# Taking a product of two tiles on GpSimd, between its gathers, instead of on VectorE

## The chip, the cores and the metric

One core of one Trainium2 chip runs the whole program. The metric is the device time of one execution, in microseconds (us). The engines are TensorE (PE in the profile; PEld is its weight load), VectorE (DVE), ScalarE (ACT), GpSimd (POOL) and SyncE (SP). "ACTq", "SPq" and "POOLq" are transfers that these engines issue to the 16 DMA engines.

## The reference, cut to what matters

The program is one layer of a streaming encoder: two attention-like branches, an output projection, and then a retrieval of experts (PEER). Only the last part is touched. For each token and each of 8 heads, two sets of 128 keys are scored, the best 16 pairs are chosen out of 128 x 128 experts, and each expert is one row of `expert_u` and one of `expert_v`:

```
fv, fi = lax.top_k(cand, P_TOPK)
eidx = jnp.take_along_axis(cidx, fi, axis=-1)
g = jax.nn.softmax(fv, axis=-1)
act = jax.nn.gelu(jnp.einsum('thkd,td->thk', expert_u[eidx], xi), approximate=False)
return jnp.einsum('thk,thkd->td', (g * act), expert_v[eidx])
```

There are 1152 tokens (1024 of the prompt and 8 streams of 16), that is nine tiles of 128 tokens, and rows of 1024 float32.

## The kernel before

The retrieval is computed in two ways at once. Six of the nine tiles are gathered: for each token the chosen rows are fetched from memory. The other three tiles (`DENSE`, 384 tokens) are dense: all 16384 experts are multiplied, as 128 groups of 128, and a matrix of gates that is zero for what was not chosen keeps the right ones.

The gathered part runs in units. A unit `q` is one tile and one head: 16 rows of `expert_u` for each token (`k` from 0 to 15) and then 16 rows of `expert_v`. GpSimd issues one indirect DMA for each of these 32 rows (L2479, 128 x 1024 float32, 512 KB), into a ring of `ROWS` = 12 buffers; the gather of row `r` first waits for `row_used`, that is until VectorE has consumed row `r - 12`. VectorE waits for each row (`row_loaded`), takes its dot product with the token (L2639, in the trace CUSTOM_DVE_ANT_0 and a short read of the accumulator) or adds it, weighted, into one of two sums (L2658 for the first two, L2661). Ahead of a unit's rows VectorE runs `choose(q + 1)`, the two rounds of top 16 and the index arithmetic for the unit that follows (L2549 to L2589). GpSimd adds the two parts of the index itself (L2473). The first three tiles (24 units) run beside the rest of the network; the dense part runs beside the last 24 units.

A dense group `e` takes these steps. ScalarE loads 128 rows each of `expert_u` (`load_u`, 512 KB, four buffers) and `expert_v` (`load_v`, 512 KB, four buffers). TensorE computes `hidden(e)`, 8 products into one PSUM bank (L2260; each appears twice in the trace, 16 records). ScalarE applies gelu to 128 x 384 values into `W[e % 4]` (L2207, `scalar_step`). `vector_step` (L2235) multiplies that tile in place with the gates of the group (`gate`, loaded for four groups at a time, 768 KB, two buffers). TensorE computes `mixed(e)`, 6 products that add up in six banks over all groups (L2269, 12 records). TensorE's own order is hidden(e), then mixed(e - 2), with `LAG` = 2.

What sets the order: each engine runs its own queue in the order of the program, and semaphores tie them. `PER_UNIT` = 5 dense groups belong to one unit, so 120 of the 128 to the 24 units, and 8 are `left` for the end. VectorE takes its five products of a unit after its dot products `k` = 4, 9 and 14 and after its weighted rows 4 and 9. ScalarE takes three of its five gelu steps, then the gelu of the unit's own dot products (L2531, which waits for all 16), then the other two, then the exponentials for the next unit (L2488, which wait for `choose`). In each step ScalarE issues `load_u(e + 4)` and `load_v(e)`, and at every fourth also the gates of the group of four that comes next, once the products of four steps back are done (`w_ready`). After the last unit VectorE takes the products of the 8 groups that are left and then, for the three dense tiles, copies the sums out of PSUM, multiplies and adds (L2690, L2676, L2678), and SyncE stores them.

Of the kernel before, what the change touches and what calls it, by code (L numbers as in the profile page):

```python
# [1819 lines left out]
class Rest:  # L1820
# [46 lines left out]
    UNITS = 2 * (NT - FIRST)  # L1867
# [262 lines left out]
ROWS = 12  # L2130
# [7 lines left out]
class Dense:  # L2138
# [88 lines left out]
            dve.tensor_tensor(self.oneB[:, b % 2], self.dT[:, d, 1, t:t + 4].unsqueeze(2).to_broadcast([P, 4, PK]),  # L2227
                              self.iota[:, 1, :].unsqueeze(1).to_broadcast([P, 4, PK]), ALU.is_equal).then_inc(self.oneB_ready, 1)

    def vector_step(self, dve, e):  # L2230
        g, jj = divmod(e, JG)
        dve.wait_ge(self.act_ready, e + 1)
        dve.wait_ge(self.gate_loaded[g % 2], g // 2 * 16 + 16)
        w = self.W[:, e % 4, :].rearrange("p (u t) -> p u t", u=12)
        dve.tensor_tensor(w, w, self.gate[:, g % 2, :, jj, :], ALU.mult).then_inc(self.w_ready, 1)  # L2235

    def tensor(self, pe):
        ps = self.ps
# [55 lines left out]
def phase_experts(nc, io, keep, later_parts, hT, branchT, modT, A2, ident, ones, score_rows, x1_rows, h2_rows, g2_rows, gate_rows):  # L2294
# [4 lines left out]
    K = TOPK  # L2299
    UNITS = NT * PH  # L2300
    tile_of = lambda q: ORDER[q // PH]
    gathered = [q for q in range(UNITS) if tile_of(q) not in DENSE]
    nth = {q: n for n, q in enumerate(gathered)}
# [3 lines left out]
    with ExitStack() as ctx:  # L2307
# [155 lines left out]

        @block.gpsimd
        def _(pool):
            for q in range(UNITS):
                if q not in nth:
                    continue
                n, j = nth[q], q % 2
                pool.wait_ge(pick_ready, n * 2 + 2)  # L2470
                if n >= 2:
                    pool.wait_ge(row_used, first_row(q) - 2 * K)
                pool.tensor_tensor(eidx[:, j, :], pick_u[:, j, 0, :], pick_u[:, j, 1, :], ALU.add).then_inc(idx_ready, 1)  # L2473
                pool.wait_ge(idx_ready, n + 1)
                for k in range(2 * K):
                    r = first_row(q) + k
                    if r >= ROWS:
                        pool.wait_ge(row_used, r - ROWS + 1)
                    pool.indirect_dma_start(rows[:, r % ROWS, :], None, io["expert_u" if k < K else "expert_v"],  # L2479
                                            bass.IndirectOffsetOnAxis(ap=eidx[:, j, k % K:k % K + 1], axis=0)  # L2480
                                            ).then_inc(row_loaded[r % ROWS], 16)

        @block.scalar
        def _(act):
# [60 lines left out]
        def _(dve):  # L2545
# [83 lines left out]
            def unit(q):  # L2629
                n, j, h = nth[q], q % 2, q % PH  # L2630
                tile = n // PH
                mine = list(steps_in(q))
                first, second = (beats(halves[2 * q + e]) if q < FIRST * PH else iter(()) for e in range(2))
                pace = [side_steps(halves[2 * q + e]) if q < FIRST * PH else 0 for e in range(2)]
                dve.wait_ge(h2_loaded, tile * 16 + 16)
                for k in range(K):
                    r = first_row(q) + k
                    dve.wait_ge(row_loaded[r % ROWS], r // ROWS * 16 + 16)
                    dve.tensor_tensor_reduce(rows[:, r % ROWS, :], rows[:, r % ROWS, :], h2[:, :], 1.0, 0.0, ALU.mult, ALU.add,  # L2639
                                             dot[:, j, k:k + 1]).then_inc(row_used, 1)  # L2640
                    if mine and k in (4, 9, 14):
                        dense.vector_step(dve, mine.pop(0))
                    for _ in range((k + 1) * pace[0] // K - k * pace[0] // K):
                        next(first)
                if q + 1 < UNITS and q != FIRST * PH - 1:
                    normalise(q + 1)
                dve.wait_ge(gelu_ready, n + 1)
                dve.wait_ge(g_ready, q + 1)
                dve.tensor_tensor(wgt[:, j, :], actv[:, j, :], g[:, j, :], ALU.mult).then_inc(wgt_ready, 1)
                dve.wait_ge(wgt_ready, n + 1)  # L2650
                if h == 0 and tile:
                    dve.wait_ge(stored, tile * 16)
                for k in range(K):
                    r = first_row(q) + K + k
                    own = acc[:, k % 2, :]
                    dve.wait_ge(row_loaded[r % ROWS], r // ROWS * 16 + 16)
                    if h == 0 and k < 2:
                        dve.tensor_scalar(own, rows[:, r % ROWS, :], wgt[:, j, k:k + 1], None, ALU.mult).then_inc(row_used, 1)  # L2658
                    else:
                        dve.wait_ge(row_used, r - 1 if k >= 2 else first_row(q))  # L2660
                        dve.scalar_tensor_tensor(own, rows[:, r % ROWS, :], wgt[:, j, k:k + 1], own,  # L2661
                                                 ALU.mult, ALU.add).then_inc(row_used, 1)
                    if mine and k in (4, 9, 14):
                        dense.vector_step(dve, mine.pop(0))
                    for _ in range((k + 1) * pace[1] // K - k * pace[1] // K):
                        next(second)
                while mine:
                    dense.vector_step(dve, mine.pop(0))

            def finish(n, sums):  # L2670
                out = acc[:, 0, :]
# [25 lines left out]
            for q in range(UNITS):  # L2697
# [15 lines left out]
                if q == FIRST * PH - 1:  # L2713
# [1 line left out]
                        pass  # L2715
                    choose(q + 1)
                    normalise(q + 1)
            for e in left:
                dense.vector_step(dve, e)
            for d in range(3):  # L2720
                dense_sums(n, d)
                n += 1
# [169 lines left out]
```

## Time and profile before

| | |
|---|---|
| three runs | 4881.58, 4904.0, 4908.69 us; median 4904.0 us |
| the profiled execution | 4896.8 us, of which 4894.9 us from the first to the last instruction |
| busy over the span | PE 75%, DVE 64%, POOL 39%, ACT 15% |
| granted clock of TensorE, mean | 0.82 |
| read and written | 1186.43 MB by DMA, 242 GB/s over the span |
| gathers | 1536, 805.40 MB, 43.4% of the DMA engines' time |

The shares are means over very different stretches. The dense part stands in the last third of the span (from about 3400 us), and only that third has the instructions that the change moves. There the page's slices show the DMA engines busy in nine tenths or more and PE too, while POOL and DVE stand at six to eight tenths.

### The profile page before, as it was taken

To read this page: it belongs to the slowest core of one execution; us is meant where nothing else is said; L and a number is where in the kernel's file an instruction comes from. 1 tells how busy PE (TensorE), PEld (TensorE's weight loads), DVE (VectorE), ACT (ScalarE), POOL (GpSimd) and SP (SyncE) were. 2 spreads that over 40 slices of the span, in tenths; PEclk is the share of its full clock that TensorE was granted. 3 is DMA by queue.
4 is the path that set the end of the run, shared out by engine and by line. 5 is a ranking of instruction groups with operands and counts; after the bars stand their busy time and mean duration, and the time that the engine had idled before them with its cause. 6 is when DMAs were issued, how large, how long until landed. Compare 5 with 4: busy or idle time off the path is not lost.

```text
span 4894.9 us, 36868 instructions
## 1 busy us (share of the span) xinstructions
PE 3684.4 (75%) x11160; PEld 2076.4 (42%) x11160; DVE 3119.7 (64%) x6614; ACT 728.7 (15%) x1215; POOL 1923.4 (39%) x1615
## 2 busy tenths in 40 slices
PE   7897879958957777437896653046999999989997
PEld 2443555345534444224453332035444444444443
DVE  1132121031128898997788757998988888888872
ACT  1032100011012333121110211034010001000000
POOL 0000000000007676776566550010777676767760
PEclk9995669958975666559998776579999999999998
DMA  6101220022358888987788782046999999999993
GB/s 246 37 29 49 97 75 26 17 78 80 92 177 316 308 329 308 350 321 276 273 315 322 261 291 87 14 140 214 388 405 408 400 409 400 409 403 406 404 408 127
DMA packets 391103, 1186.43 MB, mean 242 GB/s; under 512 B 37516, under 2 KB 124172, under 8 KB 386452
## 3 DMA queue, kind: packets, MB, share of 16 engines
q0 software_dynamic: 221184, 805.40, 43.4%
q10 hardware_dynamic: 107456, 211.61, 11.5%
q1 hardware_dynamic: 62304, 167.59, 9.9%
q8 instruction: 64, 1.05, 0.1%
q14 instruction: 95, 0.78, 0.0%
HBM read 1116.50 MB, written 67.96 MB: 242 GB/s over the span
## 4 chain that ended last, share of the span: by engine, by line
DVE 19%; PE 17%; DMA 12%; issue 11%; POOL 10%; ACT 1%; ACTq 0%; SPq 0%; DVEq 0%
POOL expert_rows L2479 10%; DMA expert_rows<-in_expert_v,expert_index 6%; DVE expert_rows L2639 3%; PE ps_all L1950 3%; DVE acc L2661 3%; PE ps_all L2250 2%; PE ps_all L1967 2%; PE ps_all L2000 2%; DMA side<-in_w_blk 2%; PE ps_all L2269 1%; DMA score_rows<-side 1%; PE ps_all L2260 1%; PE ps_all L1940 1%; DMA side<-in_w_oT 1%; DVE hot L2579 1%
## 5 line engine op out<-in xcount | busy, mean ns | idle before, releaser
L2479 POOL DMA_INDIRECT expert_rows<-in_expert_u,expert_index x768 | 935.5, 1218 | 755.4 <-DVE dots L2639 515.7
L2479 POOL DMA_INDIRECT expert_rows<-in_expert_v,expert_index x768 | 956.1, 1245 | 374.5 <-issue 227.9
L2661 DVE SCALAR_TENSOR_TENSOR acc<-expert_rows,weights,acc 128x1024 f32<-128x1024 f32 x756 | 940.4, 1290 | 144.8 <-DMA expert_rows<-in_expert_v,expert_index 142.4
L2639 DVE CUSTOM_DVE_ANT_0 expert_rows<-expert_rows,h_rows_sb 128x1024 f32<-128x1024 f32 x768 | 897.5, 1222 | 35.5 <-DMA expert_rows<-in_expert_u,expert_index 35.0
L2260 PE MATMUL ps_all<-hT,branchT 128*128 128x384 f32 x2048 | 716.9, 506 | 82.8 <-ACT side L2207 68.8
L2269 PE MATMUL ps_all<-branchT,side 128*128 128x512 f32 x1536 | 684.6, 595 | 20.1 <-DMA branchT<-in_expert_vj 16.9
L2260 PEld LDWEIGHTS ps_all<-hT,branchT 128*128 128x128 f32 x2048 | 403.9, 198 | 404.8 <-issue 180.9
L2269 PEld LDWEIGHTS ps_all<-branchT,side 128*128 128x128 f32 x1536 | 291.4, 191 | 368.8 <-issue 320.8
L1017 POOL COPY sel_head<-keep 4x128 f32 x4 | 1.1, 285 | 538.3 <-POOLq L68 436.0
L1950 PE MATMUL ps_all<-hT,side 128*128 128x384 f32 x512 | 178.1, 508 | 35.9 <-DMA side<-in_w_blk 35.9
L590 POOL COPY sel_pair<-keep 8x256 f32 x4 | 1.6, 397 | 499.6 <-POOLq L68 398.6
L2242 PE MATMUL ps_all<-consts,keep 128*128 128x128 f32 x9 | 2.7, 436 | 237.4 <-DVE keep L2710 237.4
L2488 ACT ACTIVATE gates<-best,neg_best 128x16 f32<-128x16 f32 x72 | 22.3, 310 | 1063.8 <-DVE neg_best L2570 1050.0
L2000 PE MATMUL ps_all<-hT,side 128*128 128x384 f32 x256 | 103.8, 573 | 66.8 <-DMA side<-in_w_pqT 62.1
L1950 PEld LDWEIGHTS ps_all<-hT,side 128*128 128x128 f32 x512 | 100.7, 199 | 112.5 <-issue 36.7
L2250 PE MATMUL ps_all<-keep 128*128 128x128 f32 x768 | 110.2, 287 | 48.0 <-issue 44.9
L374 PE MATMUL ps_blkA<-hT,w_ringA 128*128 128x384 f32 x384 | 126.9, 494 | 20.0 <-DMA w_ringA<-in_w_blk 20.0
L1599 PE MATMUL ps_all<-consts,side 128*128 128x128 f32 x240 | 59.5, 420 | 107.9 <-ACT side L1699 107.9
L2473 POOL TENSOR_TENSOR expert_index<-picked 128x16 uint32<-128x16 uint32 x48 | 21.4, 446 | 291.2 <-DVE picked L2585 290.4
L383 PE MATMUL ps_rowB<-w_rowsB,hT 128*128 128x512 f32 x288 | 126.8, 603 | 8.0 <-DMA w_rowsB<-in_w_row 8.0
L374 PE MATMUL ps_blkB<-hT,w_ringB 128*128 128x384 f32 x384 | 125.7, 491 | 6.3 <-DMA w_ringB<-in_w_blk 6.3
L2207 ACT ACTIVATE side<-ps_all 128x384 f32<-128x384 f32 x128 | 60.1, 488 | 424.0 <-PE ps_all L2260 423.8
(375 smaller groups left out, 5078.7 us busy)
## 6 DMA issues: line engine op xcount, KB each, us to landing
branchT<-in_expert_uT ACTq DMA_DIRECT2D x128, 512.0 KB, 7.2
branchT<-in_expert_vj ACTq DMA_DIRECT2D x128, 512.0 KB, 9.6
w_mod_ring<-in_w_mod SPq DMA_DIRECT2D x12, 2048.0 KB, 10.1
gate_rows<-branchT ACTq DMA_DIRECT2D x12, 2048.0 KB, 8.7
keep<-gate_rows ACTq DMA_DIRECT2D x32, 768.0 KB, 12.6
expert_rows<-in_expert_u,expert_index POOLq DMA_INDIRECT x768, 8.9
expert_rows<-in_expert_v,expert_index POOLq DMA_INDIRECT x768, 8.9
w_gate_ring<-in_w_blk SPq DMA_DIRECT2D x20, 512.0 KB, 3.6
```

The costliest lines, as they stand in the source:

```text
L374: mm = pe.matmul(ps[:, j, c, 0:TC], w[:, j, k, :], hT[:, k, c * TC:(c + 1) * TC], start=(k == 0), stop=(k == KD - 1))
L383: mm = pe.matmul(ps_row[:, (r * NT + t) % 2, :], hT[:, k, t * P:(t + 1) * P], wr[:, k, :], start=(k == 0), stop=(k == KD - 1))
L1950: mm = pe.matmul(ps[:, 2 * j + c, 0:TC], self.w[:, k, :], hT[:, k, (c + 1) * TC:(c + 2) * TC], start=(k == 0), stop=(k == KD - 1))
L1967: mm = pe.matmul(ps[:, 2 * j + c, 0:TC], self.w[:, k, :], mT[:, k, 0:TC], start=(k == 0), stop=(k == KD - 1))
L2000: mm = pe.matmul(ps[:, c, 0:TC], self.w[:, k, :], hT[:, k, (c + 1) * TC:(c + 2) * TC], start=(k == 0), stop=(k == KD - 1))
L2207: act.activation(self.W[:, e % 4, :], self.ps[:, e % 2, 0:TC], ACT.Gelu).then_inc(self.act_ready, 1)
L2250: mm = pe.matmul(ps[:, b % 4, n * PK:(n + 1) * PK], self.oneA[:, b % 2, n, :], self.oneB[:, b % 2, n, :], start=True, stop=True)
L2260: mm = pe.matmul(ps[:, e % 2, 0:TC], self.uT[:, e % 4, k, :], self.hT[:, k, 2 * TC:T], start=(k == 0), stop=(k == KD - 1))
L2269: mm = pe.matmul(ps[:, 2 + 2 * d + c, :], self.W[:, e % 4, d * P:(d + 1) * P], self.vj[:, e % 4, c * 512:(c + 1) * 512], start=(e == 0), s ...
L2479: pool.indirect_dma_start(rows[:, r % ROWS, :], None, io["expert_u" if k < K else "expert_v"], bass.IndirectOffsetOnAxis(ap=eidx[:, j, k % ...
L2639: dve.tensor_tensor_reduce(rows[:, r % ROWS, :], rows[:, r % ROWS, :], h2[:, :], 1.0, 0.0, ALU.mult, ALU.add, dot[:, j, k:k + 1]).then_inc ...
L2661: dve.scalar_tensor_tensor(own, rows[:, r % ROWS, :], wgt[:, j, k:k + 1], own, ALU.mult, ALU.add).then_inc(row_used, 1)
```

## The change

The product of a dense group (L2235) is issued by GpSimd and not by VectorE: `vector_step` becomes `pool_step`, with the same two waits (gelu done, gates loaded), the same operands and the same signal. In GpSimd's queue it stands right behind the gather of the row that is 12 rows after the one behind which VectorE took it: behind the gathers of weighted rows 0, 5 and 10 of the unit, and of dot rows 0 and 5 of the next one. What falls behind the last gather, and the 8 groups that are left, come at the end of the queue. VectorE's queue keeps nothing in their place.

```diff
-    def vector_step(self, dve, e):
+    def pool_step(self, pool, e):
         g, jj = divmod(e, JG)
-        dve.wait_ge(self.act_ready, e + 1)
-        dve.wait_ge(self.gate_loaded[g % 2], g // 2 * 16 + 16)
+        pool.wait_ge(self.act_ready, e + 1)
+        pool.wait_ge(self.gate_loaded[g % 2], g // 2 * 16 + 16)
         w = self.W[:, e % 4, :].rearrange("p (u t) -> p u t", u=12)
-        dve.tensor_tensor(w, w, self.gate[:, g % 2, :, jj, :], ALU.mult).then_inc(self.w_ready, 1)
+        pool.tensor_tensor(w, w, self.gate[:, g % 2, :, jj, :], ALU.mult).then_inc(self.w_ready, 1)
...
         @block.gpsimd
         def _(pool):
-            for q in range(UNITS):
-                if q not in nth:
-                    continue
+            due = {}
+            for q in gathered:
+                mine = list(steps_in(q))
+                for n, e in enumerate(mine):
+                    at = (4, 9, 14, K + 4, K + 9)[n]
+                    due.setdefault(first_row(q) + at + ROWS, []).append(e)
+            for q in gathered:
                 n, j = nth[q], q % 2
...
                     pool.indirect_dma_start(rows[:, r % ROWS, :], None, io["expert_u" if k < K else "expert_v"],
                                             bass.IndirectOffsetOnAxis(ap=eidx[:, j, k % K:k % K + 1], axis=0)
                                             ).then_inc(row_loaded[r % ROWS], 16)
+                    for e in due.pop(r, ()):
+                        dense.pool_step(pool, e)
+            for r in sorted(due):
+                for e in due[r]:
+                    dense.pool_step(pool, e)
+            for e in left:
+                dense.pool_step(pool, e)
...
-                    if mine and k in (4, 9, 14):
-                        dense.vector_step(dve, mine.pop(0))
...
-                    if mine and k in (4, 9, 14):
-                        dense.vector_step(dve, mine.pop(0))
...
-                while mine:
-                    dense.vector_step(dve, mine.pop(0))
...
-            for e in left:
-                dense.vector_step(dve, e)
```

## Rows read from the trace of the kernel before

**Rows 1.** Stage by stage: PE, PEld, DVE, ACT, POOL busy, clock, DMA share, GB/s.
```profile
3440.00:4780.00 1340.00, 1252.06 (x3282) 636.62 (x3282) 1155.23 (x2117) 122.84 (x228) 942.54 (x766) 0.97 1.02 405
```

**Rows 2.** The same columns in windows of 4 us; three units, at the weighted rows.
```profile
3658.00:3662.00 4.00, 4.00 (x10) 1.72 (x10) 3.84 (x9) 0.59 (x2) 3.13 (x3) 1.00 0.95 349
...
4007.00:4011.00 4.00, 4.00 (x11) 1.85 (x10) 3.08 (x9) 0.60 (x2) 3.08 (x4) 1.00 1.02 405
...
4121.60:4125.60 4.00, 4.00 (x11) 1.74 (x10) 3.93 (x10) 0.59 (x2) 3.09 (x4) 1.00 0.88 257
...
4702.00:4706.00 4.00, 4.00 (x13) 2.12 (x12) 4.00 (x4) 0.00 (x0) 3.09 (x3) 1.00 0.97 363
```

**Rows 3.** Waits from 3440 to 4780 us: us in total, times, longest.
```profile
POOL expert_rows L2479 <- DVE dots L2639: 158.3, 28, 12.3
...
PE ps_all L2260 <- ACT side L2207: 68.8, 20, 9.2
...
DVE acc L2661 <- DMA expert_rows<-in_expert_v,expert_index: 136.4, 135, 2.8
```

**Rows 4.** POOL in order of time: start, us; in brackets the idle time before.
```profile
3470.79 1.68 POOL L2479 DMA_INDIRECT expert_rows<-in_expert_u,expert_index  x1 [5.85 <-DVE dots L2639]
...
3980.56 0.94 POOL L2479 DMA_INDIRECT expert_rows<-in_expert_u,expert_index  x1 [0.30 <-issue]
...
3991.87 1.99 POOL L2479 DMA_INDIRECT expert_rows<-in_expert_u,expert_index  x1 [0.30 <-issue]
3994.16 1.32 POOL L2479 DMA_INDIRECT expert_rows<-in_expert_u,expert_index  x1 [0.30 <-issue]
3995.79 1.98 POOL L2479 DMA_INDIRECT expert_rows<-in_expert_u,expert_index  x1 [0.30 <-issue]
3998.07 1.98 POOL L2479 DMA_INDIRECT expert_rows<-in_expert_v,expert_index  x1 [0.30 <-issue]
```

**Rows 5.** DVE in order of time, the same unit, around one product.
```profile
3994.11 0.56 DVE L2235 TENSOR_TENSOR side<-side,keep 128x384 f32<-128x384 f32 x1
3994.58 1.22 DVE L2639 CUSTOM_DVE_ANT_0 expert_rows<-expert_rows,h_rows_sb 128x1024 f32<-128x1024 f32 x1
...
3995.73 1.22 DVE L2639 CUSTOM_DVE_ANT_0 expert_rows<-expert_rows,h_rows_sb 128x1024 f32<-128x1024 f32 x1
```

**Rows 6.** POOL's other instructions, from their lines: shortest/median/longest ns.
```profile
L1415 POOL COPY head_keys<-sub_keys x8: 295/296/297, 1391.1 to 1431.1; 128x128 f32 x8
...
L1336 POOL COPY gate_tiles<-modT x1: 1037/1037/1037, 1362.2 to 1362.2; 128x1024 f32<-128x1024 f32 x1
...
L2473 POOL TENSOR_TENSOR expert_index<-picked x48: 217/379/1842, 1464.9 to 4714.8; 128x16 uint32<-128x16 uint32 x48
```

**Rows 7.** PE and ACT in order of time, the same unit.
```profile
3988.03 7.09 PE L2260 MATMUL ps_all<-hT,branchT 128*128 128x384 f32 x16 [3.08 <-ACT side L2207]
3995.28 5.39 PE L2269 MATMUL ps_all<-branchT,side 128*128 128x512 f32 x12 [0.16 <-DMA branchT<-in_expert_vj]
4000.51 5.32 PE L2260 MATMUL ps_all<-hT,branchT 128*128 128x384 f32 x16
4005.67 5.31 PE L2269 MATMUL ps_all<-branchT,side 128*128 128x512 f32 x12
...
4009.76 0.47 ACT L2207 ACTIVATE side<-ps_all 128x384 f32<-128x384 f32 x1
```

**Rows 8.** The start of the dense part: DVE and POOL in order, one window.
```profile
3423.00 0.56 DVE L2235 TENSOR_TENSOR side<-side,keep 128x384 f32<-128x384 f32 x1 [18.53 <-DMA keep<-gate_rows]
...
3424.97 1.68 POOL L2479 DMA_INDIRECT expert_rows<-in_expert_v,expert_index  x1 [17.10 <-DVE dots L2639]
...
3430.00:3435.00 5.00, 5.00 (x16) 2.80 (x16) 5.00 (x9) 0.00 (x0) 4.39 (x3) 1.00 0.76 230
```

**Rows 9.** The end: POOL and PE in order of time.
```profile
4742.14 1.31 POOL L2479 DMA_INDIRECT expert_rows<-in_expert_v,expert_index  x1 [0.31 <-issue]
...
4741.56 5.42 PE L2269 MATMUL ps_all<-branchT,side 128*128 128x512 f32 x12 [1.91 <-DVE side L2235]
```

More of the change, by code:

```diff
@@ L2631, in unit @@
                 tile = n // PH
-                mine = list(steps_in(q))
                 first, second = (beats(halves[2 * q + e]) if q < FIRST * PH else iter(()) for e in range(2))
```

## The prediction

> **What bounds the kernel now.** I read the slices of the page first: only the last third holds the instructions that move. Then the busy time of that stage, from 3440 to 4780 us [rows 1]: the DMA engines are busy for a share of 1.02 and move 405 GB/s, while POOL is busy 943 and DVE 1155 of 1340 us. So the first suspect is DMA bandwidth, and an engine that is relieved gains nothing by itself. TensorE is busy for 1252 us, but its five groups of a unit need only ten steps of 5.16 us from start to start [rows 7], 51.6 us, and a unit lasts about 57 us (23 of them from the first dot product of the first unit to the last weighted rows; 1340 / 57 = 23.5). The difference is what it waits for ScalarE, 68.8 us in 20 waits [rows 3].
>
> Next the same stage in windows of 4 us, since a mean of 405 hides dips [rows 2]. They all lie at one place of a unit, 8 to 16 us after the gather of the first weighted row. In 10 of the 23 units the rate there falls below 400 GB/s; the first (349), one of the deepest (257) and the last (363) are shown, beside a unit that keeps 405. There the DMA engines have nothing left to do for a moment: the bound passes to whoever supplies them.
>
> The supplier is POOL. Its list in order of time shows two speeds [rows 4]: a gather takes 0.94 us and 0.30 to the next, 1.24 in all, while VectorE does little; it takes 1.32 to 1.99 us while VectorE runs dot products back to back, so 1.63 to 2.29 from start to start. For 512 KB in 2.29 us that is 229 GB/s, far under 405. The waits show the rest [rows 3]: POOL stands for VectorE 158.3 us in 28 waits, and that is one wait per unit, when its ring of 12 is full and VectorE is in `choose`; the usual one is 5.85 us [rows 4], 5.55 over the gap that is always there. So POOL has about 5.5 us of room in a unit and no more, all of it at the unit's start. VectorE waits for rows 136.4 us [rows 3], 5.9 us in a unit.
>
> **What leaves VectorE.** 128 products. From the start of one to the next instruction it is 0.47 us (3994.11 to 3994.58 [rows 5]), so 2.35 us in a unit of five. VectorE waits 5.9 us per unit for rows as it is, so this is worth nothing on the path: the wait for the rows grows by what is saved.
>
> **What POOL takes on.** No row has a 128x384 product on POOL. From below: its copies of 128 and of 1024 columns take 0.296 and 1.037 us [rows 6], so 0.83 ns for a column and 0.19 us fixed, and 384 columns 0.51 us if a second input were free. From the nearest two-input row, 0.217 us for 16 columns at its shortest [rows 6], less 0.19: 1.7 ns for a column, 0.84 us for 384. To that comes what slows the gathers: next to VectorE's two-input work one of them is held by up to 1.99 - 0.94 = 1.05 us [rows 4]. So between 0.51 and 1.89 us. I take 1.1: 0.84 and a quarter of 1.05, because a gather that has been held ends about 0.25 us ahead of VectorE's next boundary, and the product stands right behind it.
>
> The rows say that VectorE's two-input work holds POOL up; they do not say the reverse, since dot products follow one another every 1.15 us [rows 5] whatever POOL issues. The Trainium skill has a rule on it ("SBUF — State Buffer", section "Who interferes with whom"): a VectorE instruction with two SBUF inputs and a GpSimd instruction that reads SBUF exclude each other, and whichever starts first keeps the shared ports until it ends. The trace agrees for the half it can show (0.94 against 1.99 us); the other half, POOL's product in front of VectorE, would be new here and is the fourth rival below.
>
> **POOL's account.** Five products are 5.5 us. One thing comes on top: a VectorE product shifts the phase between the two engines, and that is where the short slots of 1.63 us come from (3994.16 to 3995.79 [rows 4], with the product at 3994.11 [rows 5]). Without the three products among the dot products three slots become 2.29, 2.0 us more, and VectorE's busy stretch ends 3 x 0.47 = 1.4 us earlier: 0.6 us net. Together 6.1 us against 5.5 us of room. As a sum it nearly fits, and by the sum alone nothing would be lost.
>
> **The place.** The first product of a unit stands behind the gather of weighted row 0, and that is just ahead of the dip. The room lies before that place, at the unit's start, so there the 1.1 us cannot be taken from it. In the 10 units that run dry the delay goes straight to the DMA engines: 1.1 and 0.6 us. A third part comes by way of TensorE. POOL does the product of group 0 of a unit when the gather behind which it stands is out, at 3998.07 + 1.98 + 1.1 = 4001.2 us in the unit shown [rows 4], where `mixed` started at 3995.28 [rows 7]: 5.9 us later. Then hidden of group 3 ends at 4001.2 + 2 x 5.16 = 4011.5, and ScalarE's gelu of that group, with its 1 MB of loads, moves from 4009.76 [rows 7] to about 4011.7. That is 2 us in which the engines run at 257 and not 405 GB/s [rows 2], 0.7 us. So 2.4 us in each of these 10 units. In the 13 others some backlog is left that no row measures: between nothing and all of 2.4 us, and I take half, 1.2. The sum is 10 x 2.4 + 13 x 1.2 = 40 us.
>
> **What costs nothing.** TensorE is later by 5.9 us within a unit, but it only moves its wait: ten steps are 51.6 us of 57, and its wait for ScalarE (3.08 us and a slow step of 7.09 behind it [rows 7]) becomes a wait for the product. If the unit were shorter than 51.6 us this cover would be gone. POOL's wait for gelu: queued behind it are all later gathers, and VectorE waits for those; but the gelu of a unit's first two groups is done before VectorE's own product, and POOL comes 4 to 9 us after that, so it never waits in mid-stage. ScalarE's wait for `w_ready` ahead of a load of gates asks for products four steps back: nothing. Later products move no DMA of POOL's or SyncE's but the gathers behind them, and those have the backlog of the weighted rows, where a gather takes 1.24 us [rows 4].
>
> **Both ends of the stage.** At the start VectorE stands 18.53 us for the first gates [rows 8], and POOL 17.10 us behind it. In the changed kernel VectorE goes on to consume the rows that have landed, and POOL alone waits, so that at 3424 us it finds an empty ring and issues in 1.24 rather than up to 2.29 us. For some 15 us the engines have room (230 GB/s at 3430 [rows 8]); a third of it is 5 us gained. At the end TensorE runs without a pause from `mixed` of the last unit's first group, 4741.56 us [rows 9]. It will start when POOL is done with it: 4742.14 + 1.31 + 1.1 = 4744.6, 3 us lost.
>
> **The sum.** 40 - 5 + 3 = 38 us. On the profiled execution's 4896.8 us that is 4935 us. The median of the runs shown, 4904.0, lies 7 us above that execution, inside their spread of 27 us, and I make no correction for it. A run of this kernel can tell about 0.5% from no change, 25 us.
>
> **The rivals.**
> All of it is hidden: the 13 units have backlog to spare, and what the 10 lose they get back since POOL's room grows as a unit gets longer. Then only the ends count, -5 + 3: 4895 us. For it speaks the flat 405 GB/s of [rows 1]; against it the dips. Chance 0.26.
>
> POOL becomes the bound: each product loses a full turn to VectorE and costs 1.89 us. 5 x 1.89 + 0.6 = 10.05 against 5.55 us of room makes each of 23 units 4.5 us longer, 104 us, which covers the loss at the place: 4896.8 + 104 - 2 = 4999 us. It decides from a price of 1.3 us or so, when five products pass the room and the 1.2 us. For it: gathers at 1.98 us are the rule, not the exception, in the dot products. Chance 0.15.
>
> VectorE is held up: POOL's product keeps it off for its 0.84 us. Net of the 0.47 that leaves, 5 x 0.37 = 1.85 us in a unit, 43 us in 23 if the 5.9 us of waiting hide none of it, on top of the forecast: 4978 us. The sentence on the skill above is the reason to list it. Against it: most of these products fall where VectorE waits for rows. Chance 0.08.
>
> Faster: VectorE sets the pace after all, being busy for 1155 of 1340 us [rows 1], each unit gets shorter by 2.35 us, 23 x 2.35 = 54 us, and with the ends 4841 us. It decides if the rows land as soon as VectorE frees their buffers. Against it stands a DMA share of 1.02: rows can't come sooner. Chance 0.09.
>
> **How the numbers follow.** The forecast, 4935 us, has a chance of 0.42 and its own range of 4910 to 4970, from a quarter to nearly all of the 2.4 us in the 13 units and the price at 0.84 or 1.4. The range over all reaches down to the hidden case and the spread of a run below it, 4880, and up into the POOL-bound case, 5010; outside are the faster case (0.09) and the dearest part of POOL's and VectorE's (0.06). Slower by over 0.5% is above 4921 us on this execution's scale: 0.42 less the 0.05 of it that lies lower, 0.15 and 0.08, makes 0.60. Faster by as much: 0.09. The rest, 0.31, within.
>
> **What would show it.** Right: the products on POOL's list at 0.8 to 1.4 us; the one wait for VectorE per unit shrunk from 5.85 to about nothing; dips at weighted rows 2 to 5 in nearly all units and deeper; `mixed` of a unit's first group waiting for POOL; units of 58 to 59 us. Wrong: units of 57 us with POOL's room still there (hidden), rows of POOL above 1.8 us with no wait for VectorE at all (POOL-bound), VectorE's dot products further apart than 1.15 us beside a product (VectorE held), or units under 56 us (faster). The step that I trust least is the half for the 13 units.

## The result, and the profile after

The changed kernel takes 4927.0 us in the median of 20 runs (4909.07 to 4943.87), the kernel before 4904.11 in 20 (4881.58 to 4918.86). The medians are 23 us apart. The ratio taken over all the runs is 1.0053 (about 26 us), with a 95% interval of 1.0040 to 1.0067. The profiled execution of it took 4937.08 us. Lines have moved by a few: L2483 is the gather, L2649 the dot product, L2669 the weighted row; L2235, the product, is now GpSimd's.

The page of the changed kernel: the span, busy time by engine, and the product's group.

```profile
span 4935.2 us, 36868 instructions
PE 3696.9 (75%) x11160; PEld 2073.3 (42%) x11160; DVE 3145.1 (64%) x6486; ACT 730.0 (15%) x1215; POOL 2073.2 (42%) x1743
...
L2235 POOL TENSOR_TENSOR side<-side,keep 128x384 f32<-128x384 f32 x128 | 143.4, 1121 | 83.7 <-ACT side L2207 74.5
```

The stage from 3440 to 4780 us, columns as in [rows 1]: 395 GB/s where it was 405, POOL busier by 137 us, VectorE by 5 although it does no product any more.

```profile
3440.00:4780.00 1340.00, 1225.06 (x3200) 621.08 (x3199) 1160.03 (x1975) 124.03 (x224) 1079.37 (x868) 0.95 1.01 395
```

Waits of the same stage (us in total, times, longest). Against [rows 3], POOL's standing for VectorE has shrunk from 158.3 to 65.5 us, and TensorE waits for POOL's product instead of for ScalarE.

```profile
DVE acc L2669 <- DMA expert_rows<-in_expert_v,expert_index: 129.3, 125, 3.6
...
PE ps_all L2269 <- POOL side L2235: 104.2, 22, 8.5
...
POOL expert_rows L2483 <- DVE dots L2649: 65.5, 41, 9.9
...
PE ps_all L2260 <- ACT side L2207: 10.7, 5, 5.6
```

How long is a unit? I take it from the first dot product of one unit to that of the next. The two lists of VectorE in order of time show the first dot product of the second unit in the dense part and of the last but one; 21 units lie between. Before:

```profile
3469.29 1.22 DVE L2639 CUSTOM_DVE_ANT_0 expert_rows<-expert_rows,h_rows_sb 128x1024 f32<-128x1024 f32 x1
...
4680.12 1.22 DVE L2639 CUSTOM_DVE_ANT_0 expert_rows<-expert_rows,h_rows_sb 128x1024 f32<-128x1024 f32 x1
```

After:

```profile
3473.37 1.22 DVE L2649 CUSTOM_DVE_ANT_0 expert_rows<-expert_rows,h_rows_sb 128x1024 f32<-128x1024 f32 x1
...
4714.48 1.22 DVE L2649 CUSTOM_DVE_ANT_0 expert_rows<-expert_rows,h_rows_sb 128x1024 f32<-128x1024 f32 x1
```

So 1210.8 / 21 = 57.66 us before and 1241.1 / 21 = 59.10 after. With that the 40.3 us between the two spans (4935.2 - 4894.9) fall into four parts: 8.8 us already stand at the first dot product of the dense part (3407.5 against 3398.7), ahead of everything that the change touches, and in the other profiles below this point lies anywhere from 3385 to 3416 us; the first unit is 65.9 and not 70.6 us, -4.7; the 21 units give +30.3; and from 4680.12 and 4714.48 to the end it is 214.8 and 220.7 us, +5.9. Without the first part the change costs 31.5 us in this one execution, inside the interval of the ratio (19.6 to 32.9 us).

The DMA rate in windows, three dips of the changed kernel (columns as in [rows 1]; the unit's first dot product is at 4125.5 and 4185.8 us): one at the weighted rows, as before, and one in two windows at the end of a unit, where the kernel before has none.

```profile
4149.50:4153.50 4.00, 4.00 (x13) 2.24 (x12) 3.85 (x4) 0.49 (x1) 3.08 (x4) 1.00 0.81 264
4229.80:4233.80 4.00, 4.00 (x12) 1.90 (x12) 3.60 (x11) 0.00 (x0) 3.39 (x3) 1.00 0.91 288
4233.80:4237.80 4.00, 4.00 (x12) 2.04 (x11) 3.79 (x16) 0.00 (x0) 3.33 (x4) 1.00 0.86 278
```

### The profile page after: what moved, and what is told of

It is laid out like the page before. It is cut to its first block, busy times and chain, and to the rows that moved or that the text cites. A ratio compares the mean times of both kernels' runs of the same rounds, so it can differ in the third digit from the quotient of the medians.

```text
span 4935.2 us, 36868 instructions
## 1 busy us (share of the span) xinstructions
PE 3696.9 (75%) x11160; PEld 2073.3 (42%) x11160; DVE 3145.1 (64%) x6486; ACT 730.0 (15%) x1215; POOL 2073.2 (42%) x1743
## 4 chain that ended last, share of the span: by engine, by line
DVE 23%; PE 18%; DMA 11%; issue 9%; POOL 8%; ACT 1%; SPq 0%; DVEq 0%; ACTq 0%; POOLq 0%
DVE expert_rows L2649 8%; POOL expert_rows L2483 7%; DMA expert_rows<-in_expert_v,expert_index 5%; PE ps_all L1950 3%; DVE acc L2669 3%; PE ps_all L2250 2%; PE ps_all L1967 2%; PE ps_all L2000 2%; PE ps_all L2260 1%; DMA side<-in_w_blk 1%; PE ps_all L2269 1%; DMA expert_rows<-in_expert_u,expert_index 1%; DMA score_rows<-side 1%; PE ps_all L1940 1%; DMA side<-in_w_oT 1%
## 5 line engine op out<-in xcount | busy, mean ns | idle before, releaser
L2483 POOL DMA_INDIRECT expert_rows<-in_expert_u,expert_index x768 | 951.1, 1238 | 658.3 <-DVE dots L2649 429.7
L2483 POOL DMA_INDIRECT expert_rows<-in_expert_v,expert_index x768 | 944.4, 1230 | 358.6 <-issue 206.9
L2669 DVE SCALAR_TENSOR_TENSOR acc<-expert_rows,weights,acc 128x1024 f32<-128x1024 f32 x756 | 985.3, 1346 | 141.5 <-DMA expert_rows<-in_expert_v,expert_index 138.5
L2649 DVE CUSTOM_DVE_ANT_0 expert_rows<-expert_rows,h_rows_sb 128x1024 f32<-128x1024 f32 x768 | 920.4, 1253 | 41.5 <-DMA expert_rows<-in_expert_u,expert_index 40.9
L2269 PE MATMUL ps_all<-branchT,side 128*128 128x512 f32 x1536 | 719.1, 620 | 106.1 <-POOL side L2235 106.1
L2260 PE MATMUL ps_all<-hT,branchT 128*128 128x384 f32 x2048 | 687.6, 490 | 24.4 <-DMA branchT<-in_expert_uT 13.6
L2260 PEld LDWEIGHTS ps_all<-hT,branchT 128*128 128x128 f32 x2048 | 391.6, 191 | 327.0 <-issue 91.6
L2269 PEld LDWEIGHTS ps_all<-branchT,side 128*128 128x128 f32 x1536 | 303.7, 199 | 478.0 <-issue 330.2
L2235 POOL TENSOR_TENSOR side<-side,keep 128x384 f32<-128x384 f32 x128 | 143.4, 1121 | 83.7 <-ACT side L2207 74.5
L374 PE MATMUL ps_blkA<-hT,w_ringA 128*128 128x384 f32 x384 | 126.7, 494 | 19.8 <-DMA w_ringA<-in_w_blk 19.8
```

The costliest lines, as they stand in the source:

```text
L374: mm = pe.matmul(ps[:, j, c, 0:TC], w[:, j, k, :], hT[:, k, c * TC:(c + 1) * TC], start=(k == 0), stop=(k == KD - 1))
L2235: pool.tensor_tensor(w, w, self.gate[:, g % 2, :, jj, :], ALU.mult).then_inc(self.w_ready, 1)
L2260: mm = pe.matmul(ps[:, e % 2, 0:TC], self.uT[:, e % 4, k, :], self.hT[:, k, 2 * TC:T], start=(k == 0), stop=(k == KD - 1))
L2269: mm = pe.matmul(ps[:, 2 + 2 * d + c, :], self.W[:, e % 4, d * P:(d + 1) * P], self.vj[:, e % 4, c * 512:(c + 1) * 512], start=(e == 0), s ...
```

## The experiments

Three theories stood against each other. *The place*: what counts is the first product of a unit, since it stands ahead of the dip (the prediction). *The sum*: what counts is all that POOL works in a unit, wherever it stands. *The hold*: a product of POOL that reads keeps VectorE off. The table is what the profiles gave. "Unit" is the mean of the same 21 units. "Works" is that length less the time in which POOL stood longer than the gap of 0.30 us that is always there; "stands" is that time. Both are summed over POOL's list in order of time. "Row" is the mean of a weighted row in these units. The ratios are taken over all runs of a kernel and runs of the kernel before that were taken with them; they are close to the quotients of the medians but not equal to them (e9_fill_mid: 3 us between the medians, 1.0019 or 9 us by the ratio).

| kernel | POOL works | stands | unit | row us | ratio, 95% |
|---|---|---|---|---|---|
| before | 50.6 | 7.0 | 57.66 | 1.285 | 1 |
| changed | 56.6 | 2.5 | 59.10 | 1.401 | 1.0053 (1.0040 to 1.0067) |
| e1_both | 56.3 | 2.8 | 59.09 | 1.383 | 1.0028 (1.0008 to 1.0047) |
| e2_fill | 54.2 | 3.4 | 57.67 | 1.284 | 1.0003 (0.9989 to 1.0017) |
| e3_unrelieved | 57.5 | 1.8 | 59.23 | 1.365 | 1.0049 (1.0031 to 1.0068) |
| e4_left_out | 49.4 | 8.3 | 57.66 | 1.280 | 0.9979 (0.9963 to 0.9995) |
| e5_fill_twice | 58.1 | 1.4 | 59.52 | 1.283 | 1.0094 (1.0067 to 1.0122) |
| e6_copy | 56.8 | 2.5 | 59.29 | 1.398 | 1.0071 (1.0044 to 1.0097) |
| e7_first_only | 51.9 | 6.2 | 58.06 | 1.280 | 1.0003 (0.9983 to 1.0023) |
| e8_four_only | 55.5 | 2.5 | 58.02 | 1.365 | 1.0027 (1.0006 to 1.0047) |
| e9_fill_mid | 55.5 | 2.5 | 58.00 | 1.284 | 1.0019 (1.0002 to 1.0036) |
| e10_one_and_early | 50.7 | 7.2 | 57.81 | 1.283 | 0.9997 (0.9982 to 1.0012) |
| e11_end_on_vector | 57.7 | 1.8 | 59.45 | 1.363 | 1.0062 (1.0042 to 1.0082) |
| e12_in_room | 55.8 | 4.2 | 59.99 | 1.281 | 1.0093 (1.0071 to 1.0114) |

A profile is one execution and lies up to 20 us off the median of its kernel, so a unit's length is trusted to some tenths of a us and no further. Part of that lies ahead of the dense part, but not all: from the first dot product of the dense part to the end, e1_both's profile is 28.0 us longer than that of before and e3_unrelieved's 34.7, while their ratios allow 4 to 23 and 15 to 33 us. The other profiles lie inside their intervals.

### POOL's work, and the relief of VectorE

**e1_both**: VectorE keeps its products, and POOL does a second one on spare tiles at the places of the change. **e2_fill**: the same with a fill of equal length, which reads nothing.

```diff
+    def pool_extra(self, pool, e):
+        g = e // JG
+        pool.wait_ge(self.act_ready, e + 1)
+        pool.wait_ge(self.gate_loaded[g % 2], g // 2 * 16 + 16)
+        o = e % 2 * TC
+        pool.wait_ge(self.extra, max(e - 1, 0))
+        pool.tensor_tensor(self.spare[:, o:o + TC], self.spare_in[:, 0:TC], self.spare_in[:, TC:2 * TC], ALU.mult).then_inc(self.extra, 1)
```

```diff
-        pool.tensor_tensor(self.spare[:, o:o + TC], self.spare_in[:, 0:TC], self.spare_in[:, TC:2 * TC], ALU.mult).then_inc(self.extra, 1)
+        pool.memset((self.spare, self.spare_in)[e % 2], 0.0).then_inc(self.extra, 1)
```

> VectorE keeps the real products, where they were; GpSimd takes a second product of the same shape (128x384, two inputs, on unused tiles, with the same two waits) at each place where the changed kernel has its own. So GpSimd pays, VectorE is relieved of nothing, and TensorE gets its tile as early as before. If the loss is GpSimd's delay of the gathers (the forecast): +15 to +30 us against the kernel before, about the changed kernel's +23, less what TensorE's lateness costs (7 us by the forecast) and plus the 5 us that the changed kernel gains at the start. If what counts is VectorE's time, lengthened by shared ports and no longer relieved: the relief of 71 us is missing, +60 us or more.

> As e1_both, but GpSimd fills 128x1152 numbers of unused tiles (it writes and reads nothing) instead of the second product: about as long, 1.06 us by the line through the two fills of the trace. If the loss is the time that GpSimd spends at these places: as e1_both, within 8 us. If it is the shared read ports, VectorE's row instructions at 1.22 us again and the time within 5 us of the kernel before.

POOL's and VectorE's groups of the fill (busy us, mean ns, idle before), then VectorE's of the changed kernel, all from 3440 to 4780 us:

```profile
L2238 POOL MEMSET keep<- 128x1152 f32 x118 | 127.0, 1076 | 0.1
...
L2682 DVE SCALAR_TENSOR_TENSOR acc<-expert_rows,weights,acc 128x1024 f32<-128x1024 f32 x370 | 465.2, 1290 | 127.0 <-DMA expert_rows<-in_expert_v,expert_index 125.6
L2660 DVE CUSTOM_DVE_ANT_0 expert_rows<-expert_rows,h_rows_sb 128x1024 f32<-128x1024 f32 x373 | 437.2, 1220 | 30.3 <-DMA expert_rows<-in_expert_u,expert_index 29.9
```

```profile
L2669 DVE SCALAR_TENSOR_TENSOR acc<-expert_rows,weights,acc 128x1024 f32<-128x1024 f32 x362 | 499.0, 1406 | 131.6 <-DMA expert_rows<-in_expert_v,expert_index 129.3
L2649 DVE CUSTOM_DVE_ANT_0 expert_rows<-expert_rows,h_rows_sb 128x1024 f32<-128x1024 f32 x361 | 443.0, 1285 | 35.0 <-DMA expert_rows<-in_expert_u,expert_index 34.5
```

In its one profile the second product alone makes the units as long as the change does (59.09 and 59.10 us). Over the runs it costs less: 14 us in the medians, a little under what was expected, where the change costs 23. So POOL's product alone costs something, and whether that is all of the change's loss isn't shown. Five fills of 1.08 us at the same places cost nothing, so a delay of 1.1 us ahead of the dip is not by itself what hurts. Beside the fill VectorE's instructions are as long as before (1290 and 1220 ns); beside the product of the changed kernel they are not (1406 and 1285). In e1_both the weighted rows grow too (1.383 us), the dot products hardly (1.237).

**e3_unrelieved**: the changed kernel, with an extra product of VectorE at its old places. **e4_left_out**: nobody does the product.

```diff
+    def vector_extra(self, dve, e):
+        o = e % 2 * TC
+        dve.wait_ge(self.act_ready, e + 1)
+        dve.wait_ge(self.extra, max(e - 1, 0))
+        dve.tensor_tensor(self.spare[:, o:o + TC], self.spare_in[:, 0:TC], self.spare_in[:, TC:2 * TC], ALU.mult).then_inc(self.extra, 1)
```

```diff
-            act.wait_ge(self.w_ready, e // JG * JG)
+            act.wait_ge(self.gate_loaded[(e // JG + 1) % 2], (e // JG + 1) // 2 * 16)
...
-        dve.tensor_tensor(w, w, self.gate[:, g % 2, :, jj, :], ALU.mult).then_inc(self.w_ready, 1)
...
-            pe.wait_ge(self.w_ready, e + 1)
+            pe.wait_ge(self.act_ready, e + 1)
```

> The changed kernel, and VectorE takes a product of the same shape on unused tiles at each place where it took the real one. If VectorE's relief is worth nothing, as forecast: the changed kernel's time, +20 to +30 us. If the relief hides part of the loss: up to 54 us more, +50 to +75.

> The kernel before without the product at all: TensorE multiplies the ungated values as soon as gelu is done. No engine pays. If VectorE's relief is worth nothing in mid-stage: 0 to -10 us (the wait for the first gates at the start goes, about 5 us). If VectorE sets the pace of a unit: -54 us.

The stage of both, in that order:

```profile
3440.00:4780.00 1340.00, 1234.46 (x3196) 624.65 (x3195) 1208.75 (x2084) 124.03 (x225) 1094.15 (x868) 0.95 1.01 395
```

```profile
3440.00:4780.00 1340.00, 1249.22 (x3306) 635.24 (x3305) 1108.80 (x1997) 122.05 (x228) 903.50 (x751) 0.98 1.02 404
```

VectorE's busy time moves by 100 us between them (1209 and 1109), and it decides little: with the relief taken back the changed kernel has units of 59.23 us, and without any product the unit is that of before, 57.66. e4 gains 14 us in the median; its profile shows 8 of them in the first unit (62.6 us, where no product waits for the first gates) and 2 at the end.

### How much POOL can take, and where

**e5_fill_twice** and **e9_fill_mid** fill 2304 and 1664 columns instead of 1152; **e6_copy** copies 1152.

```diff
+        pool.memset(self.spare2, 0.0).then_inc(self.extra, 1)
...
+        pool.tensor_copy(self.spare, self.spare_in).then_inc(self.extra, 1)
```

> e2_fill with twice the length: 128x2304 numbers, about 2.1 us on GpSimd at each of the places, written and nothing read; VectorE keeps the real products. If GpSimd's work in a unit is what counts (in e2_fill 32 issues of 1.53 us, five fills of 1.1 and 0.8 us make about 55 us of 57.4, and so cost nothing): about 60 us, each of 22 units 2.5 us longer, +50 to +60 us. If only reads beside VectorE's row instructions cost: within 5 us of the kernel before.

> e2_fill with 128x1664 numbers, about 1.50 us by the line through the fills of e2_fill and e5_fill_twice: chosen so that GpSimd's work in a unit, 32 issues, the index and five fills, makes 57.1 us, as in e1_both, without a read. If GpSimd's sum is what counts: as e1_both, +10 to +28 us. If it is that GpSimd's reads hold VectorE's weighted rows (1.38 against 1.28 us in e1_both): 0 to +6 us.

> As e2_fill, but a copy of 128x1152 numbers (one input) instead of the fill, 1.15 us by the line through the two copies of the trace. VectorE keeps the real products. If reads of GpSimd beside VectorE's two-input instructions cost: as e1_both, +10 to +25 us, with VectorE's row instructions longer than 1.22 and 1.28 us. If only GpSimd's time counts: within 5 us of e2_fill, that is of the kernel before.

POOL's groups, the double fill and then the copy:

```profile
L2494 POOL DMA_INDIRECT expert_rows<-in_expert_u,expert_index x368 | 438.8, 1192 | 136.1 <-issue 91.6 <-DVE dots L2661 34.2 <-POOL expert_index L2488 6.2
...
L2239 POOL MEMSET keep<- 128x2304 f32 x113 | 230.2, 2037 | 0.1
```

```profile
L2493 POOL DMA_INDIRECT expert_rows<-in_expert_u,expert_index x368 | 452.9, 1231 | 160.1 <-issue 90.5 <-DVE dots L2660 60.5 <-POOL expert_index L2487 6.2
...
L2238 POOL COPY keep<-keep 128x1152 f32<-128x1152 f32 x113 | 144.5, 1279 | 0.5
```

The fills leave VectorE's rows as long as before and so give a ladder: POOL works 54.2, 55.5 and 58.1 us in a unit, and the unit is 57.67, 58.00 and 59.52 us. So POOL's work makes units longer without holding VectorE's rows, from about 55 us on, with 2.5 us of standing still left. Two things grow together on this ladder, the sum and the length of each of the five stretches in which no gather goes out (1.08, 1.50 and 2.04 us); it doesn't tell them apart, and more but shorter fills were not tried. The fill of 1.50 us lies below what the sum was expected to give: 3 us in the medians, 9 by the ratio (1 to 18), against 10 to 28. The copy reads, is shorter than that fill, and costs more (+31 us in the medians, 1.0071). Part of that is POOL's own: its gathers beside the copy take 1.27 us in the mean and beside the fill 1.19, so it works 56.8 us and not 55.5.

**e7_first_only** leaves to POOL only the first product of each unit, the one at *the place*; **e8_four_only** leaves to it the other four and the 8 at the end.

```diff
+    def on_pool(e):
+        return e < 120 and e % 5 == 0
```

```diff
+    def on_pool(e):
+        return e >= 120 or e % 5 > 0
```

> The changed kernel with only the first product of each unit on GpSimd (behind the gather of weighted row 0), the other four and the 8 left over on VectorE. If the place ahead of the dip is what costs (the forecast): most of the changed kernel's loss, +15 to +25 us. If it is the sum of GpSimd's work: one product fits in its room of 5.5 us, and only the late start of TensorE's last stretch stays, 0 to +7 us.

> The opposite: the first product of each unit on VectorE, the other four and the 8 left over on GpSimd. If the place ahead of the dip is what costs: 0 to +8 us. If it is the sum of GpSimd's work: four fifths of it, by the account 1.1 us per unit less than the changed kernel, so 0 to +8 us as well; if it is every product that meets VectorE's rows: +12 to +18 us. With e7_first_only it tells the place from the sum: place 20 and 5, sum 3 and 5, each product alike 5 and 15.

What TensorE waited for, in e7 and then in e8:

```profile
PE ps_all L2288 <- POOL side L2246: 89.5, 23, 8.4
```

```profile
PE ps_all L2288 <- POOL side L2246: 61.2, 23, 5.6
...
PE ps_all L2279 <- ACT side L2208: 21.5, 8, 6.2
```

How deep the dips are can be added up: in windows of 4 us, the bytes that each falls short of 405 GB/s, as the time that they would take at that rate, in 21 units. At the weighted rows (16 to 32 us after a unit's first dot product) that is 11.7 us before and 24.6 changed; in the last 16 us of a unit, 0.2 and 13.7. So about half of the change's loss stands at a place where the kernel before loses nothing. The first product alone makes the dips at the weighted rows deeper (19.8 us; 0.2 at the end) and the units 0.40 us longer; the median hardly moves (+2 us), so these 0.40 us are not clear of the noise. The other four alone make these dips nearly vanish (2.1 us) and open those at the end (11.0 us): the units are 0.36 us longer, and the median is 18 us up (13 by the ratio). Of the accounts that the two runs were to tell apart, the place (20 us in e7 and 5 in e8) falls, since e7's interval is -8 to 11 us. The sum (3 and 5) and a cost for each product alike (5 and 15) both lie inside the two intervals (e8's is 3 to 23), and these runs don't decide between them. All five give 1.44, nearly twice the sum of the two. Where VectorE keeps the products and POOL does something more at the same places, nearly all of the missing time is at the end: 10.5 and 27.1 us in e1_both, 10.1 and 30.7 in e6_copy, 5.1 and 38.6 in e5_fill_twice.

**e12_in_room** takes e1 and moves all five second products behind the gather of dot row 11, where POOL stands anyway because its ring is full.

```diff
-                for n, e in enumerate(mine):
-                    at = (4, 9, 14, K + 4, K + 9)[n]
-                    due.setdefault(first_row(q) + at + ROWS, []).append(e)
+                for e in mine:
+                    due.setdefault(first_row(q) + 2 * K + ROWS - 1, []).append(e)
```

> VectorE keeps the real products. GpSimd does the same second product of 128x384 as in the run with both, five in a unit, but all five behind the gather of dot row 11 of the next unit, where it stands each time because its ring is full. So GpSimd's work in a unit is the same as there (account about 57 us), only its place in the queue is another. If the sum of GpSimd's work is what costs, wherever it stands: units of 58.4 to 58.8 us and 1.002 to 1.005 of the time of before. If the cost comes from the gathers that stand behind a product and go out late, then five products of 1.12 us fit into the 5.5 us of standing there, no gather goes out more than about 1 us late, and it is nothing: units of 57.3 to 57.7 us, GpSimd's wait behind dot row 11 gone, 0.999 to 1.001. If it is VectorE that is held by a product that reads: the products stand beside the choice of the next unit, whose instructions would be longer, and the dot products and weighted rows would go back to the means of before (1.22 and 1.28 us); units of 57.4 us plus what the choice gets longer by, up to 5 x 0.5 us.

POOL and VectorE in order of time, one unit, and in a fence of its own one instruction of `choose` in all units of the stage (shortest/median/longest ns):

```profile
4124.77 4.81 POOL L2239 TENSOR_TENSOR keep<-keep 128x384 f32<-128x384 f32 x5
4133.70 1.72 POOL L2493 DMA_INDIRECT expert_rows<-in_expert_u,expert_index  x1 [4.12 <-DVE dots L2660]
...
4126.35 3.27 DVE L2593 TENSOR_SCALAR best_pair<-best_at 128x16 uint32<-128x16 uint32 x1
4129.53 0.16 DVE L2594 TENSOR_SCALAR best_pair<-best_at 128x16 uint32<-128x16 uint32 x1
```

```profile
L2593 DVE TENSOR_SCALAR best_pair<-best_at x22: 175/3270/4516, 3464.4 to 4723.3; 128x16 uint32<-128x16 uint32 x22
```

The same instruction in the kernel before:

```profile
L2572 DVE TENSOR_SCALAR best_pair<-best_at x22: 174/175/176, 3466.5 to 4677.4; 128x16 uint32<-128x16 uint32 x22
```

The hold came nearest: its units were 57.4 us plus up to 2.5, it expected the rows at their old length (1.281 us), and the unit is 59.99. What is held it had not named. An instruction of 16 columns, 0.175 us before, stands until POOL's train of five products ends (4124.77 + 4.81 = 4129.58), and its twin behind it takes 0.16 again. `choose`, from the last weighted row to the first dot product, goes from 9.06 to 13.40 us in the median, and POOL waits for it once more. So *the hold* is real, and where it hits `choose` it is on the path: the unit is 59.99 us although POOL works 55.8, 2 us longer than e8 or e9 at nearly the same work. Whether the room could be filled with work that reads nothing was not tried as such. But in e5_fill_twice a fill, which only writes, runs into the same instruction in 4 of the 21 units, and holds it too, for up to 1.71 us:

```profile
3931.03 2.04 POOL L2239 MEMSET keep<- 128x2304 f32 x1
...
3931.39 1.71 DVE L2594 TENSOR_SCALAR best_pair<-best_at 128x16 uint32<-128x16 uint32 x1
```

### Two attempts at a better kernel

**e10_one_and_early**: VectorE does the products but the very first, which POOL takes, and ScalarE takes four gelu steps ahead of the unit's own gelu instead of three.

```diff
+    def on_pool(e):
+        return e == 0
...
-                    for e in mine[:3]:
+                    for e in mine[:4]:
...
-                    for e in mine[3:]:
+                    for e in mine[4:]:
```

> A candidate that should beat the kernel before: only the very first of the 128 products on GpSimd (so that GpSimd and not VectorE waits for the first gates; 4.7 us in the changed kernel's first unit), and ScalarE takes the fourth of a unit's gelu steps, with its 1 MB of loads, ahead of the gelu of the unit's own dot products, so that these loads fall into the dip behind the first weighted rows (12 us of missing transfers in 22 units). Both: -5 to -15 us. If the dips are not on the path: -4 us.

ScalarE's wait for the dot products falls from 328.8 us to 66.0, TensorE's wait for ScalarE stays (70.1 us, 68.8 in [rows 3]). The first unit is 68.0 us and not 70.6; the time is that of before, and the 5 to 15 us were not gained.

**e11_end_on_vector**: the changed kernel with the last unit's products and the 8 at the end on VectorE.

```diff
+    def on_pool(e):
+        return e < 115
```

> The changed kernel, with the last unit's five products and the 8 left over on VectorE. If TensorE's last stretch, which starts late when its first product waits for GpSimd, is part of the loss: 5 to 10 us less than the changed kernel, +13 to +18 us. If the loss is all in the units before: +23 us.

It gains nothing. TensorE's last wait, in the changed kernel and then here, is that for the first product of the last but one unit:

```profile
4728.06 7.11 PE L2269 MATMUL ps_all<-branchT,side 128*128 128x512 f32 x12 [4.25 <-POOL side L2235]
```

```profile
4732.46 6.92 PE L2288 MATMUL ps_all<-branchT,side 128*128 128x512 f32 x12 [4.87 <-POOL side L2246]
```

From there TensorE has no wait above 0.3 us, so what comes later on POOL or VectorE can't help it. That answers to [rows 9], where its last wait came a unit later.

## Why the prediction was right, and where it was not

Forecast: 38 us over the profiled execution of before. Measured: 40.3 us there, 31.5 of them in the part that the change touches, and 23 in the medians. The time was right; two steps of its reasons were not.

**POOL's price and account: right.** The product takes 1.121 us in the mean, taken as 1.1. POOL works 6.0 us more in a unit; the account said 6.1.

**"As a sum it nearly fits, and by the sum alone nothing would be lost": this step failed.** The ladder of fills shows that the cost begins about 2.5 us before the room is used up. POOL's room is a mean of 7.0 us, but units differ (5.85 us in the usual one, 12.3 at most [rows 3, 4]): in the changed kernel 6 of the 21 units have nothing left while the mean still has 2.5. The second place where the rate falls, at a unit's end, is worth 13.7 us of full rate in 21 units and was in no term of the sum.

**The place: a part, not the whole.** The forecast put all of 40 us, 1.7 us per unit, on the first product and nothing on the four others, "those have the backlog". Measured, the first alone gives 0.40 us per unit, the four alone 0.36, all together 1.44. Two of its three parts, the 1.1 and 0.6 us that a late gather was to cost, don't show at this place: with POOL as busy there but TensorE's tile on time (e1, e6) the dips are no deeper than before. The third part does: the gelu of a unit's group 3, with its 1 MB of loads, comes 25.2 us after the unit's first dot product in the mean where it was 21.4, so 3.8 us later and not 2, and 24.9 in e7, whose dips are deeper too (in e3 26.0, with 13.9 us missing); in e1 it is 21.9, in e8 21.3. The half for the 13 units was the step trusted least; the dips did become deeper, but in about as many units as before, not in nearly all. That the size came out is luck: too much at this place and nothing at the other offset each other.

**VectorE's relief worth nothing: right,** by e3 and e4. The list of VectorE shows besides that it isn't even relieved: its rows became longer beside POOL's products. Here a dot product beside the product of POOL, 2.00 us instead of 1.22:

```profile
4137.86 1.18 POOL L2235 TENSOR_TENSOR side<-side,keep 128x384 f32<-128x384 f32 x1
4139.18 1.78 POOL L2483 DMA_INDIRECT expert_rows<-in_expert_v,expert_index  x1
...
4136.96 1.22 DVE L2649 CUSTOM_DVE_ANT_0 expert_rows<-expert_rows,h_rows_sb 128x1024 f32<-128x1024 f32 x1
...
4138.11 2.00 DVE L2649 CUSTOM_DVE_ANT_0 expert_rows<-expert_rows,h_rows_sb 128x1024 f32<-128x1024 f32 x1
```

**The start, -5: right** (-4.7). VectorE no longer stands for the first gates; POOL does (its list), and the rate from 3430 us is 411 GB/s where it was 230 [rows 8] (the window):

```profile
3431.95 0.99 POOL L2235 TENSOR_TENSOR side<-side,keep 128x384 f32<-128x384 f32 x1 [12.11 <-ACT side L2207]
```

```profile
3430.00:3435.00 5.00, 3.41 (x10) 1.57 (x9) 1.70 (x2) 0.60 (x2) 2.60 (x3) 1.00 1.02 411
```

Of the others, the runs in which POOL has the first product (e3, e7, e10, e11) have a first unit of 66.6 to 68.0 us, those in which VectorE has it 69.9 to 72.2, and 74.2 in e12.

**The end, +3: too small** (+5.9). `mixed` of a unit's first group starts 13.6 us after the unit's first dot product where it was 7.8, 5.8 us later; the forecast said 5.9 and costed it at nothing, since TensorE has waits to spare. That holds in mid-stage. After the last but one unit there are none, and the 5.8 us fall due. The wait of 1.91 us that TensorE still had in the kernel before [rows 9] would have taken up a part, but the step behind the late start ran 7.11 us (the line under e11_end_on_vector) and not 5.31.

**The rivals.** *Hidden* and *faster* fall: units are longer. *POOL becomes the bound* was nearer the mechanism but had the wrong price (1.89 us, measured 1.121) and the wrong point from which it decides: not when five products pass the room, at a price of 1.3 us, but from about 55 us of work in the fills, and then gently. *VectorE held*: the hold is there, and so is the sign that the forecast named for it, dot products further apart than 1.15 us beside a product (the lines above), but how much of the 1.44 us it makes stays open. At POOL's work of 56.6 us the ladder of fills, read in a straight line between 55.5 and 58.1, gives a unit of 58.6; the changed kernel has 59.1. The 0.5 us that are left may be the hold, or the product's place and size; and POOL's work contains gathers that VectorE holds in turn.

## What to carry to other kernels

In this kernel the engine that issues the gathers had less room than its waits showed: compare what it works in a unit with the unit's length, and expect a cost when a few us are left, not when none is. Work that was moved to GpSimd cost twice where it read, once on GpSimd and once on the VectorE instructions beside it, so a relief of VectorE is best counted in the lengths that VectorE shows afterwards. A phase shift that waits absorb in every unit can fall due after the last wait.

## What the hardware showed unexpectedly

**The hold goes both ways, and for VectorE's rows only reading counts.** Beside products of POOL dot products rose from 1.224 to 1.285 us and weighted rows from 1.290 to 1.406 in the mean; beside fills of the same length they stayed. An integer instruction of 16 columns (a tensor_scalar) was held by reading and writing alike: 1.71 us instead of 0.175 beside a fill, until the fill ended, and 3.27 us in a train of POOL's products. The Trainium skill ("SBUF — State Buffer", section "Who interferes with whom") says that a VectorE instruction with two SBUF inputs collides with a GpSimd one that reads but not with one that only writes, that a tensor_scalar can collide too, and that whichever starts first blocks the other entirely; these rows agree. The train goes further than that sentence: the integer instruction started at 4126.35, while the second of the five products ran (0.96 us each from 4124.77), and was let in only behind the fifth.

**A pause of TensorE shows in its clock.** After it waited 6.70 us for POOL, a step of `mixed` took 8.41 us (5.39 in [rows 7]), and in the 4 us from 4141.5 the granted clock was 0.54 of full speed, so for nearly all of them the lower of its two levels, 1.2 GHz of 2.4. The list and the window:

```profile
4139.09 8.41 PE L2269 MATMUL ps_all<-branchT,side 128*128 128x512 f32 x12 [6.70 <-POOL side L2235]
```

```profile
4141.50:4145.50 4.00, 4.00 (x6) 1.54 (x5) 3.93 (x10) 0.22 (x1) 3.39 (x3) 0.54 0.93 303
```

That is 3 us more for TensorE in a unit in which it waits anyway.
